# A hybrid encoder layer on one core: attention and output projection moved from the mixer into an MLP of six token blocks

## What is computed

```python
hn = rmsnorm(x, ln1_g) * (1.0 + sc1) + sh1
z = hn @ w_in                      # 1024 -> 2832 columns, split among the heads
o_a = gated linear attention       # chunked state, chunks of 64 tokens
o_b = RG-LRU recurrence            # width-4 conv, gates, linear scan
o_c = stick_breaking(qc, k_all, v_all, q_pos, k_pos)   # causal, over all keys
o_d = short gated convolution
mix = jnp.concatenate([o_a, o_b, o_c, o_d], axis=-1) @ w_out
x = x + g1 * mix
h2 = rmsnorm(x, ln2_g) * (1.0 + sc2) + sh2
x = x + g2 * (jnp.square(jax.nn.relu(h2 @ mlp_w1)) @ mlp_w2)
y = rmsnorm(x, final_g)
```

## Time and profile before

| | us |
|---|---|
| three runs | 3482.36, 3482.82, 3483.55 (median 3482.82) |
| the profiled execution, its span | 3482.2 |
| setup, to the first block's tokens | 123 |
| four prompt blocks up to their attention | 190, 189, 189, 188 |
| their attention | 53, 122, 191, 259 |
| their output projection and the change to the next block | 58 each |
| sample | 176 |
| load and norm ahead of the MLP | 31 |
| MLP | 1539 |

### The profile page before, as it was taken

The page is one execution under the profiler, slowest core; times in us unless marked ns, Lnnn a source line. Parts: engine busy times, 40 slices in busy tenths (PEclk is TensorE's granted clock), DMA queues, the critical chain, the costliest instruction groups (busy, mean ns, idle before and its releaser), DMA issues. The chain is left out here.

```text
span 3482.2 us, 43476 instructions
## 1 busy us (share of the span) xinstructions
PE 3062.8 (88%) x15985; PEld 2660.8 (76%) x15985; DVE 1662.6 (48%) x2420; ACT 1316.4 (38%) x1876; POOL 910.7 (26%) x472
## 2 busy tenths in 40 slices
PE   4797899688977889767897699999999999999997
PEld 1475676466755667545686599999999999999997
DVE  4417215641367413677302444455655456655555
ACT  3436335543455434455312422223532225432222
POOL 0231233023300233000200433334633326522330
PEclk9899899788977889777855799999999999999998
DMA  7231323022300223000241422222232121222210
GB/s 260 87 111 41 97 61 97 1 70 64 103 18 0 69 64 103 18 0 0 88 125 43 148 73 67 66 72 61 73 128 72 60 72 54 81 94 72 72 60 34
DMA packets 305776, 251.06 MB, mean 72 GB/s; under 512 B 10747, under 2 KB 268134, under 8 KB 305638
## 3 DMA queue, kind: packets, MB, share of 16 engines
q1 hardware_dynamic: 287238, 219.30, 21.0%
q10 hardware_dynamic: 18400, 29.89, 2.4%
HBM read 223.13 MB, written 21.70 MB: 70 GB/s over the span
## 5 line engine op out<-in xcount | busy, mean ns | idle before, releaser
L1658 DVE SCALAR_TENSOR_TENSOR xs<-op,modT,xs 128x352 f32<-128x352 f32 (+1 forms) x896 | 454.7, 528 | 201.5 <-PE op L1753 199.9
L1732 PE MATMUL hp<-h_hi,w1h 128*128 128x352 f32 x1536 | 497.5, 324 | 13.6 <-POOL h_lo L1482 13.6
L1751 PE MATMUL op<-g_hi,w2h 128*128 128x352 f32 x1536 | 501.0, 326 | 1.5 <-DVE xs L1658 1.1
L1733 PE MATMUL hp<-h_lo,w1h 128*128 128x352 f32 x1536 | 496.8, 323 | 0.0
L1734 PE MATMUL hp<-h_hi,w1l 128*128 128x352 f32 x1536 | 496.0, 323 | 0.0
L1752 PE MATMUL op<-g_lo,w2h 128*128 128x352 f32 x1536 | 495.1, 322 | 0.0
L1753 PE MATMUL op<-g_hi,w2l 128*128 128x352 f32 x1536 | 494.5, 322 | 0.0
L610 POOL TENSOR_TENSOR w_lo<-wraw,w_hi 128x1024 fp32r<-128x1024 f32 x122 | 297.1, 2436 | 461.6 <-ACT w_hi L646 452.5
L1471 POOL TENSOR_TENSOR w1l<-w1r,w1h 128x1024 fp32r<-128x1024 f32 x96 | 230.5, 2402 | 616.5 <-ACT w1h L1513 616.5
L1116 PE MATMUL zp<-hn_hi,w_hi 128*128 128x512 f32 x960 | 383.5, 399 | 2.4 <-POOL w_lo L610 1.8
L1120 PE MATMUL zp<-hn_lo,w_hi 128*128 128x512 f32 x960 | 376.4, 392 | 2.5 <-POOL hn_lo L627 2.5
(11 more groups left out here) (256 smaller groups left out, 4531.8 us busy)
## 6 DMA issues: line engine op xcount, KB each, us to landing
wraw<-in_w_in_dram SPq DMA_DIRECT2D x96, 512.0 KB, 3.8
w1r<-in_mlp_w_dram SPq DMA_DIRECT2D x96, 512.0 KB, 4.1
w2r<-in_mlp_w_dram SPq DMA_DIRECT2D x96, 512.0 KB, 3.3
wraw<-in_w_out_dram SPq DMA_DIRECT2D x34, 512.0 KB, 4.0
wada<-in_w_ada_dram ACTq DMA_DIRECT2D x6, 2048.0 KB, 9.7
wada<-in_w_ada_dram SPq DMA_DIRECT2D x6, 2048.0 KB, 8.7
xs<-x_scratch SPq DMA_DIRECT2D x3, 2816.0 KB, 12.2
oT<-in_x_prompt_dram SPq DMA_DIRECT2D x4, 2048.0 KB, 7.9
```

Of the source, the lines that this page charges most:

```text
L1658: ins = dve.scalar_tensor_tensor(out=cols, in0=op[i % 4][:, a:e], scalar=modT[:, M_G2 + d, m:m + 1], in1=cols, op0=ALU.mult, op1=ALU.add)
L1732: pe.matmul(bank, w1h[ft][:, k, :], h_hi[:, k, cols], start=(k == 0), stop=False)
L1733: pe.matmul(bank, w1h[ft][:, k, :], h_lo[:, k, cols], start=False, stop=False)
L1751: pe.matmul(bank, wh, g_hi[odd][:, ft, cols], start=(ft == 0), stop=False)
```

## The change

The mixer no longer does prompt attention or the output projection. Heads A, B and D go to DRAM as hi and lo halves (`o_scratch`), and so do q, k and v (`q_scratch`, `k_scratch`, `v_scratch`) and the transposed tokens (`x_scratch`). A new `trunk_phase` takes the place of `mlp_phase`. It runs six token blocks of 352 (`NMB`, `TB`). A block is: 8 strips of `w_out`, the norm, then 8 chunks of 4 hidden tiles each (`FPC`), each chunk projecting the chunk before. Between these ticks, `walk` lets each engine do steps of the prompt attention, at a rate that `Pace` sets: 30 steps for token block 0 at once and up front, 46 spread over MLP block 0, 140 over MLP blocks 1 to 3. One step handles one head, 128 queries and up to 512 keys, in stages: scores at step s, exp at s+2, transposes at s+6, values at s+7. The whole phase is written out, with no loop.

A weight tile is split anew for each block of 352 tokens. `g_lo` is made on POOL, `op` has two banks, raw weights have a ring of three tiles, and the final norm is done row-wise on ACT and DVE.

```diff
-def mlp_phase(nc, const, x1_v, mlp_w1, mlp_w2, y_prompt, y_sample):
...
+    def block(self, m):
+        left = sum(STEPS[:2]) - self.done if m == 0 else sum(STEPS) - self.done
+        units = 112 if m == 0 else 120 * (4 - m) - 8 + 16 * (3 - m) if m < 4 else 1
+        self.rate = left / units
...
+def walk(pace, out_strip, rms, hidden, project, turn):
+    for m in range(NMB):
+        pace.finish(NEEDS[m])
+        for d in range(KT):
+            out_strip(m, d)
+            if 0 < m < 4:
+                pace(2)
+        if m:
+            project(m - 1, NCH - 1, 0)
+            project(m - 1, NCH - 1, 1)
+        rms(m)
+        if m:
+            for d in range(2, KT):
+                project(m - 1, NCH - 1, d)
+        pace.block(m)
+        for c in range(NCH):
+            for j in range(FPC):
+                hidden(m, c, j)
+                pace(2)
...
+            if c:
+                for d in range(KT):
+                    project(m, c - 1, d)
+                    pace(1)
...
+        # POOL
+            def after_strip(m, c, j):
+                g = strip_no(m, c, j)
+                if g + 2 < NMB * STRIPS_PER:
+                    lo_first(g + 2)
+                if c is None and j < FPC and m:
+                    lo_second(m - 1, NCH - 1, j)
+                if c:
+                    lo_second(m, c - 1, j)
...
+            def hidden(m, c, j):
+                after_strip(m, c, j)
+                i = FPC * (NCH * m + c) + j
+                odd = c % 2
+                pool.wait_ge(gh_ready, i + 1)
+                pool.tensor_tensor(g_lo[odd][:, j, :], sqt[i % 2][:, :], g_hi[odd][:, j, :].bitcast(F32),
...
+        # ACT
+            def hidden(m, c, j):
...
+                hp_read(act, u)
+                wait(act, h_sq, i - 1)
+                act.activation(rt[i % 2][:, :], hp[u % 2][:, 0:TB], ACT.Relu).then_inc(hp_free[u % 2], 1)
+                after_strip(m, c, j)
+                act.wait_ge(h_sq, i + 1)
...
+        # PE
+            def project(m, c, d):
+                n, odd = KT * (NCH * m + c) + d, c % 2
+                if d == 0:
+                    pe.wait_ge(gh_ready, FPC * (NCH * m + c + 1))
+                    pe.wait_ge(gl_ready, FPC * (NCH * m + c + 1))
+                    pe.wait_ge(w_hi, second[m, c, FPC - 1] + 1)
+                    pe.wait_ge(w_lo, second[m, c, FPC - 1] + 1)
+                wait(pe, o_added, n - 1)
```

More of the change, by code:

```diff
@@ L502, in shape_of, with attend @@
             return (DEC, 1, 1, DEC) if sample else (BLK, TPB, CPB, P)
[L504 to L514, removed]
+        def attend(key_block):
+            key_block(0, lambda s: DEC, True, 1)
+            key_block(2, lambda s: PAST, False, 0)
         @block.sync
@@ L843, in body @@
-                if not sample:
-                    act.wait_ge(norm_done, KT * b + 2 * NORM_C)
-                    for i in range(3):
+                    act.wait_ge(ot_full, 1)
+                    act.activation(oT[:, 4:6, 0:n], tp2[:, :, 0:n], ACT.Copy).then_inc(ot_done, 1)
+                    act.wait_ge(ot_done, 1)
+                    norm_squares(NORM_C)
+                    act.wait_ge(nsum_full, 3 * b + NORM_C + 1)
+                    norm_ln(NORM_C)
+                    norm_exp(NORM_C)
@@ L1297, in body @@
                 norm(NORM_C)
-                if sample:
-                    pe.wait_ge(norm_done, KT * (b + 1))
-                for i in range(N_IN_STRIPS, N_STRIPS):
-                    strip(i)
             def turn_states(i):
@@ new lines, in raw_order, with after @@
+def raw_order():
+    first, second, n = {0: 0, 1: 1}, {}, itertools.count(2)
+    def after(g, m, c, j):
+        if g + 2 < NMB * STRIPS_PER:
+            first[g + 2] = next(n)
+        if c is None and j < FPC and m:
+            second[m - 1, NCH - 1, j] = next(n)
+        if c:
+            second[m, c - 1, j] = next(n)
+    for g in range(NMB * STRIPS_PER):
+        m, i = divmod(g, STRIPS_PER)
+        after(g, m, None if i < KT else (i - KT) // FPC, i if i < KT else (i - KT) % FPC)
+    for j in range(FPC):
+        second[NMB - 1, NCH - 1, j] = next(n)
+    return first, second
@@ L1459, in _, with load_raw @@
-            store_rows(NSB - 1)
-            for i in range(2):
-                sp.wait_ge(y_out[i], 16 * NSB * len(TILES) // 2)
+            strips = {r: g for g, r in first.items()}
+            rows2 = {r: key for key, r in second.items()}
+            state = {"next": 0}
+            def load_raw():
+                r = state["next"]
+                if r >= len(first) + len(second):
+                    return
+                state["next"] = r + 1
+                slot = raw[r % RAW]
+                wait(sp, w_hi, r - RAW + 1)
+                wait(sp, w_lo, r - RAW + 1)
+                if r in strips:
+                    m, i = divmod(strips[r], STRIPS_PER)
+                    src = wout_v[:, :, i * P:(i + 1) * P] if i < KT else w1_v[:, :, (i - KT) * P:(i - KT + 1) * P]
+                    sp.dma_start(slot[:, :, :], src).then_inc(raw_in[r % RAW], 16)
+                else:
+                    m, c, j = rows2[r]
+                    row = (FPC * c + j) * P
+                    sp.dma_start(slot[:, :, :].rearrange("p k n -> p (k n)"), mlp_w2[0, row:row + P, :]
+                                 ).then_inc(raw_in[r % RAW], 16)
@@ new lines, in _, with out_strip @@
+            pace = Pace(attention())
+            def after_strip(m, c, j):
+                load_raw()
+                if (c is None and j < FPC and m) or c:
+                    load_raw()
+            def out_strip(m, d):
+                if d == 0 and m == 0:
+                    load_o(0)
+                after_strip(m, None, d)
+            def hidden(m, c, j):
+                after_strip(m, c, j)
+                if (m, c, j) == (NMB - 1, NCH - 1, FPC - 1):
+                    while state["next"] < len(first) + len(second):
+                        load_raw()
@@ L1717, in _ @@
+            walk(Pace(attention()), out_strip, rms, hidden, project, turn)
         @block.tensor
         def _(pe):
[L1719 to L1735 removed]
```

1197 lines of the change are left out of this document (707 added, 490 removed).

## The result

The changed kernel takes **3881.43 us** (median of 4 runs, 3876.31 to 3883.83) against 3482.59 for the kernel before beside it: a ratio of 1.114, 95% interval [1.1127, 1.1158]. It is slower, as forecast; 4160 was too much by 279 us, 7%, and rival 1's 3740 too little by 141. The profiled execution spans 3879.9 us.

What follows compares the result with a forecast made beforehand. PE bounds the MLP before; in the trunk POOL's remainders hold up each projection. First phase 1140 plus trunk 3023 (2410 chunks, 390 sections, 148 start, 75 row turns and end) made 4163, say 4160 us; range 3720 to 4560.

Steps and rivals of the forecast that it cites:

- rival 1: Trunk: only POOL's work sets the pace, DVE slips between its instructions, steps hide in PE's waits; 3740 us, chance 0.17.
- first phase: Before the trunk: 1025 us kept from before plus 115 for uncovered loads, roundings, ACT's transfers; ends at 1140 (1070 to 1200).
- block 0's start: Trunk start: loads 12, 30 uncovered attention steps 65, store and load 14, strips 36, norm and halves 21; 148 us.
- chunks: MLP blocks: seven chunks each, 58.3 us with attention or 46.3 without, plus a first one of strips alone; 2410 us.
- sections between blocks: Between MLP blocks: `w_out` strips, norm, projections shared with halves on DVE; 86 us three times, 66 twice, 390.
- row turns and end: Trunk: row turns 25 us and the end 50, outside the chunks; 75 us.
- The row shows it passed on only where POOL pauses, and I go by the row: DVE's squares beside POOL's remainders: the shared port waits for POOL's pause; otherwise a chunk would be some 3 us shorter.
- the restart of the clock: PE after its wait ahead of the projections: about 3.2 us at half speed, 1.6 us lost a chunk.
- 17 x 0.7 = 12: Attention steps in a chunk of blocks 0 to 3: 17 us at full weight, 0.7 on the mean, so 12 us added.
- the bound of 3990: Lower bound of the total if a step costs only PE's 1.5 us: 6 instead of 12 us in 28 chunks.
- each projection 0.6 + 4 x 0.69, not 1.92: Between blocks: projections shared with eight halves on DVE take this long each, behind strips and norm; sections 86 or 66 us.
- Rival 2: Trunk: PE stays full, remainders ready in time, steps fit beside; faster, 3230 us, chance 0.06.

Runs made afterwards that it cites:

- Late `w1l`: Changed kernel, with POOL's `w1l` for the next chunk's first two strips moved behind the `w2l` of strip 3: 3747.2 us, 1.0756 of before.
- early `w2l`: Late `w1l` kernel, with each second-layer tile split one place earlier and none behind strip 3: 3673.6 us, 1.0553 of before.
- late `g_lo`: Early `w2l` kernel, with POOL's `g_lo` moved behind the last `w2l` and a third tile for the square: 3660.8 us, 1.0519 of before.
- the steps at the borders: Changed kernel, with no attention step between ticks; each block's attention done in one piece where needed at the latest: 4262.7 us, 1.2234 of before.
- the five waits moved: Late `g_lo` kernel with all steps among projections, plus row turns behind the third projection and four groups of loads moved ahead: 3480.0 us, 1.0004 of before.

## Why the prediction was right, and what in it was not

The terms, forecast and measured (from the first relu's times; chunks include the first ones of strips alone, and a block's seventh full chunk is taken at the mean of its six pitches):

| term | forecast | measured |
|---|---|---|
| first phase | 1140 | 1145 |
| block 0's start | 148 | 170 |
| chunks | 2410 | 2236 |
| sections between blocks | 390 | 291 |
| row turns and end | 75 | 38, the end alone: the row turns lie in the chunks |
| sum | 4163 | 3880 |

- **The direction and the place were right.** PE waits for the `w2l` made behind strip 3, POOL's remainders lie in one unbroken run ahead of the projection, and POOL rests during it. Late `w1l`, early `w2l` and late `g_lo` show the cause by taking it away piece by piece, with the same products on PE: chunks 4 to 6 of blocks 4 and 5 take 45.4, 40.8, some 36 and 33.6 us. PE's wait, 8.1 us on the mean, is shorter than the "10 to 17" forecast: in the chunk shown PE is done with strip 3 some 16 us behind the end of strip 0, not 14, and the gate ends earlier.
- **The chunk without steps: 46.3 forecast, 45.3 measured,** but partly for a wrong reason. The step that failed is "The row shows it passed on only where POOL pauses, and I go by the row". The gate was to be 25.6 us from the end of strip 0; it is 1.7 + 22.2 = 23.9, rival 1's 24.2. Of the 192 squares, 121 took over 0.7 us, and all of these ended 0.38 or 0.39 us behind the end of the POOL instruction then running; in 107 of the cases POOL's next instruction followed at once. The one of 3230.98 above ended at 3233.27, where `w2l` ended at 3232.89, and the `g_lo` that follows on POOL lasts 1.24 instead of 0.93. The Trainium skill ("SBUF — State Buffer", "SBUF: two separate sides") has the lock held for the whole instruction, and these rows agree. Squares of "3 to 5 us" did not come: 1.31 on the mean. Rival 1, which had this part right, left out the restart of the clock, which the forecast had: 1.6 against 1.7 measured.
- **The rows of before did not decide it.** The trace of before has 92 squares over 0.7 us. In 88 of them POOL paused behind the instruction that the square waited for, and such a row fits both readings. In the other four the next remainder followed at once. Three of these squares waited for that one too, the one of the earlier trace rows and those of 2907.88 (3.05 us) and 3003.91 (3.27 us); one, of 2502.15, did not. Three `g_lo` of DVE in the same place did not either, the first of them:
```profile
1978.52 5.33 POOL L1474 TENSOR_TENSOR w2l<-w2r,w2h 128x1024 fp32r<-128x1024 f32 x2
...
1979.51 2.08 DVE L1643 TENSOR_TENSOR g_lo<-sqt,g_hi 128x352 fp32r<-128x352 f32 x1 [0.56 <-ACT g_hi L1530]
...
2905.80 4.75 POOL L1474 TENSOR_TENSOR w2l<-w2r,w2h 128x1024 fp32r<-128x1024 f32 x2
...
2907.88 3.05 DVE L1640 TENSOR_TENSOR sqt<-rt 128x352 f32<-128x352 f32 x1 [3.78 <-ACT rt L1526]
```
  This `g_lo` ends at 1981.59, some 0.4 us behind the first half of POOL's pair, which lasts until 1983.85; the square ends at 2910.93, 0.38 behind the whole pair. So the forecast's reading had three rows for it and four against it in that trace. Why the three squares missed their turn stays open. They began 0.32 to 0.54 us before the running instruction ended, but so did squares that were let in: the one of 2502.15 began 0.53 us before, the one of 3235.95 above some 0.46.
- **The chunk with steps: 58.3 forecast, 53.3 measured.** The term "17 x 0.7 = 12" was mis-sized: it is 8.0. Its split (7 among strips, 10 among projections) fell too, as the two runs with all steps at one place cost a chunk about the same. Its "234 steps" are 216 (30 + 46 + 140), which hardly moves the term. Scans were to take "well over 1.27"; those of full width took 1.36 in block 2:
```profile
L1898 DVE TENSOR_TENSOR_SCAN t_cc<-t_lt,t_carry 128x512 f32<-128x512 f32 x20 | 27.2, 1362 | 0.7
```
  With the forecast's 5.8 steps a chunk, 8.0 is 1.4 us a step, near the 1.5 of PE's own work that gave the bound of 3990. The windows above show the same: PE is busy 40.9 and 40.0 us a chunk in blocks 0 and 2 against 34.6 in block 4, so PE's own work is most of what a step adds. Rival 1 would have it hidden in PE's waits for POOL, but these do not shrink: 350.4 us on `w2l` with the steps among the ticks, 346.3 with the steps at the borders.
- **Sections: 390 forecast, 291 measured.** Behind blocks 0 to 2 they are 73, 51 and 64 instead of 86, behind 3 and 4 49 and 55 instead of 66. The step that was mis-sized is the one that adds strips, norm and halves one behind the other ("each projection 0.6 + 4 x 0.69, not 1.92"); that they overlap is argued from the sum, no run took it apart.
- **Block 0's start: 148 forecast, 170 measured.** The two waits for transfers were mis-sized: 25.9 us for attention's first loads ("loads 12") and 20.7 for the heads ("its store and load 14").
- **The first phase held.** It ends at 1145 instead of 1140. At a border the transfers take 16 us from the first store's issue to the tokens' landing, where 13 was taken and 20 the bound: beside the heads' store the tokens land after 12.1 us, not 7.9.
- **Rival 2** stayed far off: the last `w2l` alone keeps PE waiting, as said against it. That its premise was sound once the gate is gone is shown by the 33.6 us chunks; but with the five waits moved the steps still cost 11.4 us a chunk, so even that version only draws level.

What stays open: with the gate gone a step costs 1.9 us (11.4 by 6.0 steps), more than the PE work in it. The waits for `a_lo` and for `op`'s adds point at DVE's order; no run tested it. No run undid the halving of the blocks either.

## What to carry to other kernels

When a change halves the tile that shares a weight, add up the preparation of that weight *in the window in which it can run*, not over the whole loop: POOL had 23.5 us of work in 45 and was the bound all the same, because it stood ahead of one gate. Work with a later deadline (here `w1l` and `g_lo`) belongs behind the gate, which was worth over 200 us with no work saved. And before a long row becomes a rule, look for all rows in which the two readings differ: here seven squares and `g_lo` of the trace of before did, three on one side and four on the other, and a single one had been read.

## What was not expected of the hardware

In the changed kernel every square on DVE (two inputs in SBUF) that waited for POOL was let in at the end of POOL's running instruction (121 of 121 over 0.7 us, in 107 of them ahead of a POOL instruction that followed at once), and POOL paid for it: the remainder beside it took some 0.28 us longer (2.65 to 2.7 against 2.35 to 2.4). In the kernel before three squares waited for a second remainder as well, and what sets them apart is not known. Moving three subtractions of 0.95 us from POOL to DVE shortened POOL's gate by 1.5 us only (22.2 to 20.7). In the chunk shown PE's granted clock was 0.57 on the mean of the 4 us behind a pause of about 8 us, then 1.00; at the MLP's start in before it was 0.68 on the mean of the first 5 us.
